# Last block's mixing stage: state space inputs taken from the unnormed hidden state, its normed split made behind them, and copies, shares and output banks moved a step ahead

## The reference, cut to what matters

```python
h = h + 0.5 * swiglu(rms_norm_2(h, ffn1_norm[i]), ...)
u = rms_norm_2(h, mix_norm[i])                # h * rsqrt(mean(h*h) + eps) * g
z = u @ w_in[i]
q, k, v, s_in, gates = jnp.split(z, splits, axis=-1)
y_attn = neighbourhood_attention(q, k, v, na_rpb[i]) @ w_attn_out[i]   # 8 heads of 64, softmax over a window
y_ssm = s5_branch(s_in, ...) @ w_ssm_out[i]   # bidirectional state space scan over 512 positions, then a GLU
g_attn, g_ssm = jnp.split(jax.nn.sigmoid(gates), 2, axis=-1)
h = h + (g_attn * y_attn + g_ssm * y_ssm) @ w_out[i]
```

## Time and profile before

| | |
|---|---|
| median of 3 runs | 3765.01 us |
| profiled execution, its span | 3767.7 us, 3765.9 us |
| PE busy | 3559.4 us, 95% of the span |
| mixing stage of the second block | about 2827 to 3277 us of the span |
| PE idle in it, as listed by who was waited for | about 45 us between 2815 and 3420 us |

### The profile page before, as it was taken

The page is one execution under the profiler, slowest core; times in us unless marked ns, Lnnn a source line. Parts: engine busy times, 40 slices in busy tenths (PEclk is TensorE's granted clock), DMA queues, the critical chain, the costliest instruction groups (busy, mean ns, idle before and its releaser), DMA issues.

```text
span 3765.9 us, 49832 instructions
## 1 busy us (share of the span) xinstructions
PE 3559.4 (95%) x20100; PEld 3048.2 (81%) x20100; DVE 2428.1 (64%) x2965; ACT 986.3 (26%) x1707; POOL 2059.5 (55%) x1100
## 2 busy tenths in 40 slices
PE   7999898999999999989889999999998998999997
PEld 7898788899999879867667778877887774688886
DVE  6686898777832657689887883287325654653325
ACT  4305542122110330543212111011003443322201
POOL 4355334566666535533446776677665552466664
PEclk9899998999999989989899999999999998999999
DMA  3122111222323312211112342233234441222231
GB/s 135 46 90 73 45 50 58 67 86 95 125 89 101 107 51 90 74 45 45 62 67 91 138 141 99 101 129 136 97 104 164 153 149 56 79 95 95 100 103 71
DMA packets 96898, 348.30 MB, mean 92 GB/s; under 512 B 10848, under 2 KB 13152, under 8 KB 93664
## 3 DMA queue, kind: packets, MB, share of 16 engines
q1 hardware_dynamic: 80064, 289.44, 22.8%
q10 hardware_dynamic: 16672, 56.70, 3.9%
HBM read 322.32 MB, written 23.79 MB: 92 GB/s over the span
## 4 chain that ended last, share of the span: by engine, by line
PE 63%; DVE 26%; ACT 6%; issue 3%; DMA 0%; POOL 0%; ACTq 0%; DVEq 0%; POOLq 0%
PE acc L480 19%; PE acc L481 19%; PE acc L483 18%; DVE cu L1991 10%; PE aux L631 1%; DVE rh L1945 1%; PE aux L782 1%; DVE ptmp L2149 1%; DVE rb L1942 1%; DVE fpr L1743 1%; DVE sm L1892 1%; DVE mtmp L1797 1%; PE acc L811 1%; PE aux L790 1%; DVE pcp L2149 1%
## 5 line engine op out<-in xcount | busy, mean ns | idle before, releaser
L453 POOL TENSOR_SCALAR whi<-raw 128x1024 fp32r<-128x1024 f32 x548 | 630.5, 1151 | 1632.6 <-PE acc L483 1611.5
L455 POOL TENSOR_TENSOR wlo<-raw,whi 128x1024 fp32r<-128x1024 f32 x548 | 1429.1, 2608 | 45.7
L480 PE MATMUL acc<-nhi,whi 128*128 128x512 f32 (+1 forms) x2776 | 956.0, 353 | 52.0 <-DVE mt L2000 22.3
L481 PE MATMUL acc<-nlo,whi 128*128 128x512 f32 (+1 forms) x2776 | 946.8, 350 | 0.0
L483 PE MATMUL acc<-nhi,wlo 128*128 128x512 f32 (+1 forms) x2776 | 868.0, 348 | 0.0
L480 PEld LDWEIGHTS acc<-nhi,whi 128*128 128x128 f32 x2776 | 526.4, 190 | 140.7 <-issue 54.0
L480 PE MATMUL acc<-bhi,whi 128*128 128x264 f32 (+1 forms) x1864 | 558.4, 316 | 38.7 <-DVE merged L2060 13.2
L481 PEld LDWEIGHTS acc<-nlo,whi 128*128 128x128 f32 x2776 | 526.0, 189 | 69.0
L481 PE MATMUL acc<-blo,whi 128*128 128x264 f32 (+1 forms) x1864 | 547.7, 310 | 0.0
L483 PEld LDWEIGHTS acc<-nhi,wlo 128*128 128x128 f32 x2776 | 487.1, 190 | 68.0
L1991 DVE SCALAR_TENSOR_TENSOR cu<-cx,par,cu 128x528 f32<-128x528 f32 (+1 forms) x480 | 490.7, 1084 | 0.0
(11 more groups left out here) (361 smaller groups left out, 4500.0 us busy)
## 6 DMA issues: line engine op xcount, KB each, us to landing
raw<-in_w SPq DMA_DIRECT2D x548, 512.0 KB, 3.3
kept_cp<-pcp ACTq DMA_DIRECT2D x4, 1280.0 KB, 6.6
cp<-kept_cp ACTq DMA_DIRECT2D x4, 1280.0 KB, 8.8
kept_ap<-pap ACTq DMA_DIRECT2D x4, 1024.0 KB, 4.1
kept_cs<-pcs ACTq DMA_DIRECT2D x4, 1024.0 KB, 6.4
ap__140<-kept_ap ACTq DMA_DIRECT2D x4, 1024.0 KB, 6.3
cs__151<-kept_cs ACTq DMA_DIRECT2D x4, 1024.0 KB, 5.5
merge_gates<-gout ACTq DMA_DIRECT2D x16, 256.0 KB, 3.4
```

What stands on the lines that cost most here:

```text
L453: pool.tensor_scalar(hi, w, 1.0, 0.0, ALU.mult, ALU.add).then_inc(sem("w_hi"), 1)
L455: pool.tensor_tensor(lo, w, hi.bitcast(F32), ALU.subtract).then_inc(sem("w_split"), 1)
L480: pe.matmul(acc[s][:, f, 0:TH], hi, xh[:, f * TH:(f + 1) * TH], start=a, stop=False)
L481: pe.matmul(acc[s][:, f, 0:TH], hi, xl[:, f * TH:(f + 1) * TH], start=False, stop=False)
```

## The change

Norm 5 joins `SPLIT_EARLY`, so the `sin2` tiles run on the split of h\*g; DVE, not ACT, evacuates them, and multiplies by 1/rms (`frs2`). After the last of them h is multiplied again, now with 1/rms (`rescaled`, into a new buffer `ftmp2`), and split again into `nhi` and `nlo` (`normed_high` on ACT, `normed_low` on DVE) for q, k, v and the gates; the first of those tiles takes each chunk as it comes. `splits(i)` counts the two splits of norm 5. The buffer `us` has two halves, and round r+1's inputs are copied in round r, between its last powers and its last gate tiles. In the attention the division of item j+1 (`share`) stands directly behind the scores of item j+2, ahead of `part`, `bar` and the gate product; item 0's stands ahead of half of the z work, and its transposed copy has a buffer of its own (`pts2_first`). Output pairs alternate between two banks (`t % 2`). The gate's 0.5\*tanh + 0.5 is folded: one instruction (tanh + 1) \* y, and the factor 0.5 is taken in the splits of the merged result, with a 2.0 on the attention's product.

```diff
@@ SPLIT_EARLY, buffers
+        frs2, o = at("frs2", [P, S], place_of_q + 2 * 4 * S * 4)
+        ftmp2, o = at("ftmp2", [P, 2, S], o)
+        pts2_first, _ = at("pts2_first", [P, 4, P], 8 * 2 * P * 4)
-        us, _ = at("us", [P, 4, NC], o)
+        us, o = at("us", [P, 2, 4, NC], o)
-        SPLIT_EARLY = {1, 2, 3, 4, 6, 7}
+        SPLIT_EARLY = {1, 2, 3, 4, 5, 6, 7}
+        def splits(i):
+            return (i + (i > 5)) * KD
@@ PE
                 def values(j):
-                        pe.wait_ge(evac[1], ph.nth(hh // 2))
+                        pe.wait_ge(evac[1], ph.nth(max(hh // 2 - 1, 0)))
...
                 for i in range(4):
                     if i == 3:
                         turn_powers(0, (0, 1))
-                    tile(AT["sin2"], i, R(nhi, nlo, S), S, each=("norm_lo", 5 * KD) if i == 0 else None)
+                    tile(AT["sin2"], i, R(nhi, nlo, S), S, each=("norm_lo", splits(5)) if i == 0 else None)
+                    if i == 0:
+                        sumsq(5)
...
                     lags(r)
-                    tiles(to_states)
+                    if r == 0:
+                        tile(AT[to_states[0]], 0, R(nhi, nlo, S), S, each=("norm_lo", splits(5) + KD))
+                    else:
+                        tiles(to_states)
@@ ACT
+                act.wait_ge(sem("na_turned"), 1)
+                act.activation(pts2_first[:, :, :], aux[1][:, 0, :].rearrange("p (a b) -> p a b", a=4), ACT.Copy)\
+                   .then_inc(sem("na_pt"), 1)
                 z_high(2)
                 exps(1)
...
-                for i in range(4):
-                    block_done(ph.block(i) + 1)
-                    act.activation(halves(uin[:, i], S), accv(ph.slot(i), S), ACT.Copy).then_inc(evac[ph.slot(i)], 1)
...
+                act.wait_ge(evac[ph.slot(0)], ph.nth(0) + 1)
+                back_cs(0)
+                copy_inputs(0, range(4))
+                repeat_b(0)
+                copy_powers(0, (0, 1))
                 act.wait_ge(sem("ss_rep"), 2)
                 back_bb(1)
+                copy_powers(0, (2, 3))
+                block_done(ph.block(3) + 1)
+                for j in range(5):
+                    normed_high(j)
...
-                    if r:
-                        copy_inputs(r, range(4))
                     act.wait_ge(sem("ss_lags"), r + 1)
...
                     m.then_inc(sem("ss_t_forward"), 1)
+                    if r == 0:
+                        for j in range(5, KD):
+                            normed_high(j)
...
                     evacuate(between_powers)
                     if r < 3:
                         copy_powers(r + 1, (2, 3))
+                        copy_inputs(r + 1, range(4))
@@ DVE
+                def share(j):
+                    b = j % 3
+                    dve.wait_ge(sem("na_exp"), j + 1)
+                    then(dve.reciprocal(sc2[:, 3, b:b + 1], sc2[:, 2, b:b + 1]))
+                    dve.tensor_scalar(na_scores(j), na_scores(j), sc2[:, 3, b:b + 1], None, ALU.mult).then_inc(sem("na_p"), 1)
...
                 score(1)
+                share(0)
                 z_product(2)
...
                     if j + 2 < len(items):
                         score(j + 2)
+                    if j + 1 < len(items):
+                        share(j + 1)
...
-                        then(dve.tensor_scalar(g, g, 0.5, 0.5, ALU.mult, ALU.add))
                         block_done(mg.block(hh) + 1)
-                        dve.tensor_tensor(halves(merged2[:, hh], S), accv(0, S), halves(g, S), ALU.mult).then_inc(evac[0], 1)
+                        dve.scalar_tensor_tensor(halves(merged2[:, hh], S), halves(g, S), 1.0, accv(0, S), ALU.add, ALU.mult)\
+                           .then_inc(evac[0], 1)
...
+                def rescaled(j):
+                    if j >= 2:
+                        dve.wait_ge(sem("norm_lo"), splits(5) + KD + j - 1)
+                    dve.scalar_tensor_tensor(ftmp2[:, j % 2], hview(S)[:, j], col("mix2_g", None, j), frs2[:, :], ALU.mult, ALU.mult)\
+                       .then_inc(sem("norm_scaled"), 1)
+                def normed_low(j):
+                    dve.wait_ge(sem("norm_hi"), splits(5) + KD + j + 1)
+                    dve.tensor_tensor(nlo[:, j, 0:S], ftmp2[:, j % 2], nhi[:, j, 0:S].bitcast(F32), ALU.subtract)\
+                       .then_inc(sem("norm_lo"), 1)
...
+                rstd(5, frs2)
+                for i in range(4):
+                    block_done(ph.block(i) + 1)
+                    dve.tensor_tensor(halves(uin[:, i], S), accv(ph.slot(i), S), halves(frs2[:, :], S), ALU.mult)\
+                       .then_inc(evac[ph.slot(i)], 1)
+                    if i == 2:
+                        rescaled(0)
+                        rescaled(1)
```

94 lines of the change are left out of this document (43 added, 51 removed).

## The result

| | before | after |
|---|---|---|
| median, beside each other on one chip | 3763.89 us (4 runs, 3762.45 to 3766.05) | 3738.46 us (4 runs, 3737.87 to 3743.72) |
| profiled execution, its span | 3767.7 us, 3765.9 us | 3738.9 us, 3737.1 us |

The ratio is 0.994, with a 95% interval of 0.9928 to 0.9953: faster by 25.4 us in the medians. The forecast was 3737. The two profiled executions lie 28.8 us apart, because that of before came out 3.8 us above its median and that of after 0.5 above its own.

The account below looks back on a forecast made before the run. PE, busy 95% of the span, was taken as the bound. Norm 9, rounds 5, attention's steady state 10.5 and start 3.5 sum to 28 us: 3737 against the median of 3765.0, range 3725 to 3750.

Parts of the forecast that it names:

- Part A: Norm, from the last addition to h to the end of `states(0)`: 53.5 us becomes 44.3, gain 9, bounds 4 to 15.
- rival 2: Second split in `qkv0` costs more or lowers the clock, some 5 us lost: 3742; chance 0.20 shared with rival 3.
- Part B: Rounds, inputs copied a round ahead: PE's `tm_` waits shrink, gain 5 us, bounds 0 and 9.
- Round 0: Input copies fit beside two gate tiles, but 0.5 us of a DMA wait reaches PE: gain 2.0 us.
- rounds 1 and 2: With one gate tile the evacuation comes 3 to 4 us late; each round still gains about 1 us.
- rival 3: Rounds give nothing back, as late `cs_` replaces the copies: 3742; chance 0.20 shared with rival 2.
- Part C, steady state: Attention's later items: waits for shares and the second bank go nearly whole, 10.5 of 11.3 us; bounds 6 and 11.3.
- Part C, start: Before `turn(1)`: hole moves one item on, 5 us gained, shrinking to 3.5 as items 1 to 3 run slowly.
- rival 1: Attention's start: clock stays up or returns fast, items 1 to 3 take 3.55 us, 7 us more, 3730; chance 0.12.
- The slower rival: Attention stays at 1.2 GHz behind its hole, 2.97 us per item; half the items slow gives 3785; chance 0.03.

Follow-up runs that it names:

- d_pieces: Changed kernel with round 1's input copies behind the first evacuation and rounds 2 and 3's in halves in ACT's idle gaps; 3733.62 us, ratio 0.9919.
- a_norm: Changed kernel with the rounds' input copies and the attention edits undone, so the norm's edits alone; 3753.97 us, ratio 0.9974 to the kernel before.
- h_late_share: Changed kernel with the shares, except item 0's, behind the other work again; 3753.83 us, ratio 0.9974 to the kernel before.
- g_one_bank: Changed kernel with one output bank for all head pairs; 3742.86 us, ratio 0.9949 to the kernel before.
- b_copies: Kernel before with only the inputs copied a round ahead; 3760.10 us, ratio 0.999.
- c_attention: Kernel before with only the attention edits: early shares, two banks, own buffer for the first transposed block, folded gate; 3750.21 us, ratio 0.9967.
- f_lows: Changed kernel with all eight chunks of the second split ahead of the additions to `tm_`; 3741.22 us, ratio 0.9944 to the kernel before.
- e_hole: Changed kernel with item 2's score and item 1's share moved ahead of the last z work; 3739.51 us, ratio 0.9938 to the kernel before.
- j_filler: `d_pieces` with in effect one gate tile moved from ahead of `outputs(3)` to ahead of `turn(0)`; 3726.70 us, ratio 0.9905 to the kernel before.
- d_pieces_again: The same kernel as `d_pieces`, on the chip of `j_filler`; 3732.62 us, ratio 0.9922 to the kernel before.

## Why the prediction was right

By its steps, with the profiled executions where a place is meant:

- **Part A, 9 forecast; 7.8 measured in the trace (45.7 us for 53.5 to the end of `states(0)`; 7.9 to its start), 9.3 in the median of the part alone.** The mechanism came as described: no wait for the sum, the second split at 1.39 us a chunk, six waits within `qkv0` (4.8 us, some 6 forecast), additions ahead of chunks 6 and 7, and the last `nlo` 39.7 us behind the addition, as forecast. What the trace lacks is the clock: it was 0.84 in 2860 to 2865 and 0.81 in 2865 to 2870, and chunks 6 and 7 took 2.7 us where the sum had 1.4. That is rival 2's mechanism, small, inside `qkv0` and gone by the rounds. The first `nlo` beside POOL, 1.35 us, came as the prediction weighed it, but within the 4 us put for the start of the second split.
- **Part B, 5 forecast; 2.1 in the trace, 3.2 in the median of the part alone.** Round 0 was right (2.5 for 2.0). The step that failed is rounds 1 and 2: I put the load of `cs_` 3 us later (it was 2.75 and 2.8 later, counted from `states(1)` and `states(2)`) and its duration at 8.4 us or less, so that each round would gain 1. The load took 9.4 and 9.0 us, the second 2.85 more than in before, and both rounds lost 1.0. That is rival 3's mechanism in two rounds of three; `d_pieces` shows it, by taking it away. The clock gave 1.6 back at the end, for the 1 forecast, but not as forecast: the hole ahead of `states(3)` didn't go, it grew from 2.07 to 2.36, and this time the clock stayed up. `a_norm` has that hole unchanged, 2.07, and full speed behind it. So this term is luck, and without it the four rounds gave 0.5.
- **Part C, steady state, 10.5 forecast; 8.6 measured.** Waits for shares and for the bank were 11.3 and are 3.2, so 8.1 went. What stays is a share stretched by POOL once a head, which the sum had not. Heads are 14.74 apart, not 14.2. `h_late_share` puts 9.6 on the order of the shares (1.1 of it a longer hole, 1.9 the clock), and `g_one_bank` 4 on the bank, more than the 2.0 of the waits before: the two don't simply add to what the waits of before had.
- **Part C, start, 3.5 forecast; 7.7 measured to `turn(4)`.** The idle time before `turn(1)` was 5.18 us (about 5 forecast), `turn(1)` came 4.8 earlier (5 forecast), and the clock fell behind it as forecast. But it was low for one item and a small part of a second, not three: rival 1 in part. The 3.5 has no working of its own: by the rows, one more slow item than before takes 2.97 from the 5, which leaves 2. `a_norm` shows why this was mis-sized: I took the 18 us of before for a property of the items, and the same items behind the same hole did it in 6, and so, within an item, did all the others with a hole of 5 to 7 us (`b_copies`, `c_attention`, `d_pieces`, `f_lows`, `g_one_bank`, `h_late_share`). The profiled execution of before was the exception, and its extra 5.9 us (8.7 for 2.7) stand in the 28.8. How much of them is in the 25.4 isn't shown: that execution lies only 3.8 above its median.
- **Sum.** B gave 2.9 us less than forecast, A 1.1 and the steady part 1.9 less, the start 4.2 more; with 2.1 ahead of the stage and 0.4 behind it, these are the 28.8 of the two profiled executions. By the medians 28 was forecast and 25.4 came. That the sum came so near is in part luck: misses of both signs cancel, and the gain at the attention's start and the last 1.6 us of the rounds hang on how long the clock was low in one profiled execution of before. The parts alone give 9.3, 3.2 and 13.1, where the prediction had 9, 5 and 14.

The slower rival (attention at half clock throughout) is not seen in any of the ten runs: behind every hole ahead of the attention, of 2.2 to 7.1 us, one or two items were slow, and later only item 17 of `h_late_share`; only the profiled execution of before had three.

## What to carry to other kernels

When work is moved off a path, look at what is queued behind its new place on the same engine: here a load, issued 3 us later, took the place of the copies, and putting the same copies into the engine's idle gaps gave 9.2 us in the rounds and not 2.1. A hole in front of a stage that the producing engine can't shorten was here better filled with a tile from elsewhere than narrowed: narrowing it from 5.2 to 2.2 us gave nothing, filling it down to 0.5 gave the idle time and the clock's loss. One profiled stretch at a low clock is no measure of how long it will last; take it from several executions before a term of a sum rests on it.

## What the runs showed of the hardware beyond this

- **The length of a low clock varies for the same instructions.** Behind the hole ahead of the attention the items ran slowly for 18 us in before (hole 7.08), 6 us in `a_norm` (7.09), about 7 in after (5.18), and 13 in `e_hole` (2.17). In these runs it does not follow the size of the hole. The Trainium skill (TensorE: Matmul & The Clock Gate, "The HAM clock gate") has the throttle released within some microseconds of sustained activity; `a_norm` and after agree, before and `e_hole` took longer. What decides between them stays open: no run here took it apart.
- **Whether a hole of 2 to 3 us brings the clock down at all varies too.** PE waits 2.0 to 2.8 us ahead of a `states` 17 times in the profiled executions of before, after and the runs. Behind six of these waits `states` took 5.2 to 5.4 us (before 2.07, `a_norm` 2.51, `c_attention` 2.07, `e_hole` 2.81, `f_lows` 2.05, `h_late_share` 2.16), behind the other eleven 3.81 (`a_norm` 2.07 and after 2.77 among them). A gain or loss of 1.6 us at one such place, in one execution, so says nothing of an edit.
- **A DVE operation with one SBUF input is stretched by POOL too.** The division of a share (128x512, one tensor in, one out) takes 0.49 us alone, and 1.27 in after and 1.35 in `j_filler` when it starts beside one of POOL's splits.
- **The load of `cs_` and m (1.5 MB on ACT's queue) for rounds 1 to 3 was ready 6.2 to 9.6 us behind its issue, and not always at the same distance in the same round.** Between rounds 1 and 2 it was 8.4 in before and `d_pieces_again`, 6.7 in `d_pieces`, 9.4 in after and 9.6 in `a_norm`, whose order of work in the rounds is that of before. Between rounds 2 and 3 it was 6.2 to 6.4 in the kernels without late copies, and 8.8 to 9.5 in those with them. The gate's output DMA stands half a microsecond ahead of it in all of them, so that is not the reason. No run was made to find it.
